# One-core transformer and Hyena block: the value projection computed by token, with key and query preparation under it, and modulation sums closed by a multiplication with ones

## What is computed

```python
mod = c_act @ mod_w[i] + mod_b[i]                      # 12 x 1024 outputs per layer
h_lat = modulate(rms_norm(x, norm_mix_g[i]), sh1, sc1) # 256 x 2048
qa, qb, ka, kb, va, vb = split(h_lat @ w_in)           # queries 2048, keys 512, values 512 columns
qb, kb = rms_norm(qb, q_norm), rms_norm(kb, k_norm)    # per head, only group B
qa, ka, qb, kb = rope(qa), rope(ka), rope(qb), rope(kb)
ka_c, kb_c, va_c, vb_c = split(h_ctx @ w_in[:, Q_WIDTH:])
kb_c = rms_norm(kb_c, k_norm)
```

## Time and profile before

| | |
|---|---|
| median of 3 runs | 2728.9 us (2728.77 to 2733.31) |
| profiled execution, its own time | 2730.95 us |
| its span, first to last instruction | 2729.2 us |
| TensorE busy | 2526.8 us, 93% |
| VectorE busy | 1995.0 us, 73% |
| ScalarE busy | 1120.9 us, 41% |
| data moved by DMA | 608.80 MB, mean 223 GB/s |
| mean granted clock of TensorE | 0.963 of full |

### The profile page before, as it was taken

The page is one execution under the profiler, slowest core; times in us unless marked ns, Lnnn a source line. Parts: engine busy times, 40 slices in busy tenths (PEclk is TensorE's granted clock), DMA queues, the critical chain, the costliest instruction groups (busy, mean ns, idle before and its releaser), DMA issues.

```text
span 2729.2 us, 41835 instructions
## 1 busy us (share of the span) xinstructions
PE 2526.8 (93%) x13492; PEld 2111.7 (77%) x13492; DVE 1995.0 (73%) x2373; ACT 1120.9 (41%) x1494; POOL 0.2 (0%) x4
## 2 busy tenths in 40 slices
PE   7869987797999999999979999999899999999996
PEld 2338884476788888888868788787688888888885
DVE  6788758777987878878768888878675565565654
ACT  2224225643444444444434334233344444444442
POOL 0000000000000000000000000000000000000000
PEclk9989997898999999999999999999899999999998
DMA  8857843474998888888858567576556666666662
GB/s 312 301 187 264 298 159 108 139 259 165 314 311 278 283 278 279 276 283 280 274 172 280 182 226 257 167 252 201 176 181 189 187 190 185 190 186 188 189 185 92
DMA packets 441695, 608.80 MB, mean 223 GB/s; under 512 B 18363, under 2 KB 387228, under 8 KB 439580
## 3 DMA queue, kind: packets, MB, share of 16 engines
q1 hardware_dynamic: 440188, 598.53, 66.9%
q10 hardware_dynamic: 1440, 9.44, 0.9%
HBM read 597.41 MB, written 10.49 MB: 223 GB/s over the span
## 4 chain that ended last, share of the span: by engine, by line
PE 82%; DVE 11%; issue 3%; ACT 2%; DMA 2%; DVEq 0%; SPq 0%; ACTq 0%
PE ps L356 47%; PE ps L365 24%; PE ps L1114 2%; DVE w_lo L395 1%; PE ps L663 1%; PE ps L929 1%; DVE acc L407 1%; PE ps L893 1%; DMA raw<-in_mlp_w 1%; PE ps L1124 1%; DVE hm L715 1%; DVE hm L723 1%; DMA raw<-in_mod_w 1%; DVE lat L729 1%; DVE sm L1508 1%
## 5 line engine op out<-in xcount | busy, mean ns | idle before, releaser
L395 DVE TENSOR_TENSOR w_lo<-raw,w_hi 128x1024 fp32r<-128x1024 f32 x720 | 877.2, 1224 | 523.5 <-ACT w_hi L391 519.3
L391 ACT ACTIVATE w_hi<-raw 128x1024 fp32r<-128x1024 f32 x720 | 760.0, 1060 | 1056.2 <-PE ps L365 892.2
L356 PE MATMUL ps<-lat,w_hi 128*128 128x512 f32 x3200 | 839.2, 399 | 65.6 <-DVE lat L729 58.5
L356 PEld LDWEIGHTS ps<-lat,w_hi 128*128 128x128 f32 x3200 | 587.3, 192 | 177.5 <-issue 49.7
L356 PE MATMUL ps<-alt,w_hi 128*128 128x512 f32 x2688 | 698.2, 395 | 7.8 <-DVE mod L419 5.7
L356 PEld LDWEIGHTS ps<-alt,w_hi 128*128 128x128 f32 x2688 | 488.1, 190 | 96.7 <-DVE mod L419 6.0
L365 PEld LDWEIGHTS ps<-lat,w_lo 128*128 128x128 f32 x3200 | 448.7, 192 | 32.0 <-DVE w_lo L395 0.4
L365 PE MATMUL ps<-lat,w_lo 128*128 128x256 f32 x3200 | 464.1, 284 | 0.0
L365 PEld LDWEIGHTS ps<-alt,w_lo 128*128 128x128 f32 x2688 | 374.7, 191 | 25.8
L365 PE MATMUL ps<-alt,w_lo 128*128 128x256 f32 x2688 | 389.1, 283 | 0.0
L407 DVE SCALAR_TENSOR_TENSOR acc<-slab,silu,acc 128x1024 f32<-128x1024 f32 x300 | 381.4, 1279 | 5.9 <-DMA slab<-in_mod_w 2.4
(11 more groups left out here) (180 smaller groups left out, 1411.6 us busy)
## 6 DMA issues: line engine op xcount, KB each, us to landing
raw<-in_mlp_w SPq DMA_DIRECT2D x512, 512.0 KB, 3.8
slab<-in_mod_w SPq DMA_DIRECT2D x352, 512.0 KB, 6.0
raw<-in_hy_w_in SPq DMA_DIRECT2D x96, 512.0 KB, 6.3
raw<-in_attn_w_in SPq DMA_DIRECT2D x48, 512.0 KB, 6.1
raw<-in_mod_w SPq DMA_DIRECT2D x32, 512.0 KB, 7.4
raw<-in_attn_w_out SPq DMA_DIRECT2D x32, 512.0 KB, 4.8
raw<-in_hy_w_out SPq DMA_DIRECT2D x32, 512.0 KB, 6.6
spec_dram<-spec ACTq DMA_DIRECT2D x8, 1024.0 KB, 7.8
```

What stands on the lines that cost most here:

```text
L356: e.matmul(ps[:, bank, :], w_hi[:, n % RING, kk, fb * P:(fb + 1) * P], t[:, kb, :], start=(kb == 0), stop=False)
L391: e.activation(w_hi[:, n % RING], raw[:, n % RING], ACT.Copy).then_inc(hi_ready, 1)
L395: e.tensor_tensor(w_lo[:, n % RING], raw[:, n % RING], w_hi[:, n % RING].bitcast(F32), ALU.subtract).then_inc(split_ready, 1)
```

## The change

The key projection stays one iteration, T_K. The value projection T_V gets its own loop, `pe_values`: now the token blocks (128 tokens, high or low part) are the stationary operand and the weights stream past, 512 columns at a time. A unit holds 2 feature blocks x 512 columns, is loaded as such, and meets four token blocks in four banks (4, 5, 0, 1); the result has tokens on partitions, as attention needs it, and is copied to `v` by four copies. The transposes of the values and `vt` go. Banks 2, 6 and 7 are free for the preparation of keys and queries, which is hung under the units of T_V by `under_values(n)` on TensorE (n = 1, 2, 4, 5, 6), ScalarE (n = 4, 6, 7) and VectorE (n = 4, 5, 6); its temporaries now lie in `sum_sb` and `lo_sum`. All sums over partitions of `acc` (17 calls of `pe_finish`, four chunks in the start) are now matmuls with a column of ones into one bank: 8 per half, and in the start 8 more per half that add `rows` through a column of the identity. The reductions over the free axis go.

The diff, cut to its core (the body of `under_values` on TensorE is the moved code of L970 to L1004 with its waits and other banks):

```diff
+        k_sq = sum_sb[:].rearrange("p a b t -> p (a b) t")
+        q_sin = lo_sum[:, 0]
...
+        def value_unit(buf, n):
+            return buf[:, n % RING].rearrange("p (k a) n -> p k (a n)", k=2)
+        def sp_values(e, T, w, col, sl):
+            for n in range(8):
+                e.wait_ge(split_ready, 8 * T + n - 3)
+                src = w[2 * n * P:2 * (n + 1) * P, col:col + 4 * HEAD]
+                e.dma_start(value_unit(raw, n), src.rearrange("(k p) n -> p k n", p=P)
+                            ).then_inc(unit_landed[n % RING], 16)
+                if n >= 4:
+                    sp_slabs(e, sl, 1, (n - 4) * 4, 4)
...
+        V_BANKS = (4, 5, 0, 1)
+        def pe_values(e, T, after_unit):
+            for n in range(8):
+                hi, lo = value_unit(w_hi, n), value_unit(w_lo, n)
+                e.wait_ge(hi_ready, 8 * T + n + 1)
+                if n == 0:
+                    e.wait_ge(psum_free, 2 * T_K + 1)
+                for kk in range(2):
+                    kb = 2 * n + kk
+                    for part in range(2):
+                        for tb, bank in enumerate(V_BANKS):
+                            act = (lat, alt)[tb // 2][:, kb, ds(part * TOK + tb % 2 * P, P)]
+                            e.matmul(ps[:, bank, :], act, hi[:, kk, :], start=(kb == 0 and part == 0), stop=False)
+                e.wait_ge(split_ready, 8 * T + n + 1)
+                for kk in range(2):
+                    kb = 2 * n + kk
+                    for tb, bank in enumerate(V_BANKS):
+                        act = (lat, alt)[tb // 2][:, kb, ds(tb % 2 * P, P)]
+                        mm = e.matmul(ps[:, bank, :], act, lo[:, kk, :], start=False, stop=(kb == KB - 1))
+                mm.then_inc(units_done, 1)
+                after_unit(n)
...
-        def pe_finish(e, sl_count, fin, n_acc):
+        def pe_finish(e, sl_count, fin, n_acc, bank=4):
             e.wait_ge(slabs_used, 4 * sl_count + 4)
             e.wait_ge(mod_ready, fin + 1)
             for h in range(n_acc):
                 for b in range(half):
-                    mm = e.transpose(ps[:, 4 + 2 * h + b // 4, (b % 4) * P:(b % 4 + 1) * P],
-                                     acc[:, h, b * P:(b + 1) * P], ident)
+                    at = h * half + b
+                    mm = e.matmul(ps[:, bank, at:at + 1], acc[:, h, b * P:(b + 1) * P], ones[:, 0:1],
+                                  start=True, stop=True)
             mm.then_inc(mod_cols, 1)
...
-        def dve_finish(e, fin, dests):
+        def dve_finish(e, fin, dests, bank=4):
             e.wait_ge(mod_cols, fin + 1)
-            for h in range(len(dests)):
-                ins = e.tensor_reduce(mod_part[:, h], ps[:, 4 + 2 * h:6 + 2 * h, :].rearrange("p a (b k) -> p (a b) k", k=P),
-                                      AX.X, ALU.add)
-            ins.then_inc(mod_summed, 1)
-            e.wait_ge(mod_summed, fin + 1)
             for h, at in enumerate(dests):
-                ins = e.tensor_tensor(mod[:, ds(at, half)], mod_part[:, h], vec("mod_b", at, half), ALU.add)
+                ins = e.tensor_tensor(mod[:, ds(at, half)], ps[:, bank, h * half:(h + 1) * half], vec("mod_b", at, half),
+                                      ALU.add)
             ins.then_inc(mod_ready, 1)
...
+        class Values(Readout):
+            def act_head(self, e, T, g):
+                if g == 1:
+                    e.wait_ge(units_done, 8 * T + 8)
+                    for tb, bank in enumerate(V_BANKS):
+                        e.activation(v[:, tb], ps[:, bank, :], ACT.Copy).then_inc(v_ready, 1)
+                    e.sem_inc(lo_copied, 2)
+            def dve_head(self, e, T, g):
+                if g == 1:
+                    e.wait_ge(v_ready, 4)
+                    e.sem_inc(psum_free, 2)
...
-            sp_call(e, T_KV, 2, a["attn_w_in"], 0, KV_COL, SL_KV)
-            e.wait_ge(split_ready, 8 * (T_KV + 2))
+            sp_iter(e, T_K, a["attn_w_in"], 0, KV_COL, 0, SL_KV)
+            sp_values(e, T_V, a["attn_w_in"], KV_COL + KV_HEADS * HEAD, SL_KV)
+            e.wait_ge(split_ready, 8 * (T_V + 1))
...
-                            e.transpose(ps[:, 4 + 2 * w + b // 4, (b % 4) * P:(b % 4 + 1) * P],
-                                        (acc, acc_odd)[par][:, w, b * P:(b + 1) * P], ident)
-                    for b in range(half):
-                        mm = e.transpose(ps[:, 0, 2 * b:2 * b + 2], rows[:, b * P:(b + 1) * P], ident[0:2, 0:2])
+                            out = ps[:, 4, w * half + b:w * half + b + 1]
+                            e.matmul(out, (acc, acc_odd)[par][:, w, b * P:(b + 1) * P], ones[:, 0:1],
+                                     start=True, stop=False)
+                            mm = e.matmul(out, rows[:, b * P:(b + 1) * P], ident[0:2, w:w + 1],
+                                          start=False, stop=True)
                     mm.then_inc(start_turned, 1)
...
-            with e.Fori(0, 2) as i:
-                pe_iter(e, T_KV + i, lat, lambda j: (norm_ready, 5 + j), alt)
-            e.wait_ge(psum_free, 2 * (T_KV + 2))
-            pe_finish(e, M_ATT, FIN_KV, 2)
+            pe_iter(e, T_K, lat, lambda j: (norm_ready, 5 + j), alt)
+            def under_values(n):
+                if n == 1:
+                    e.wait_ge(psum_free, 2 * (T_K + 1))
...
+            pe_values(e, T_V, under_values)
+            pe_finish(e, M_ATT, FIN_KV, 2, 3)
             e.wait_ge(mod_ready, FIN_KV + 2)
...
-            for h in range(KV_HEADS):
-                for tb in range(4):
-                    mm = e.transpose(ps[:, h, tb * P:(tb + 1) * P], vt[:, h, tb * P:(tb + 1) * P], ident)
-                mm.then_inc(vt_turned, 1)
...
-            act_iter(e, T_KV, r, KeysValues(kt))
-            act_iter(e, T_KV + 1, KeysValues(kt), KeysValues(vt))
-            act_flush(e, T_KV + 1, KeysValues(vt))
-            for h in range(2):
-                e.wait_ge(psum_free, 2 * (T_KV + 2))
-                e.activation(k_sq[:, 2 * h:2 * h + 2, :].rearrange("p a t -> p (a t)"), kt[:, 2 + h, :],
-                             ACT.Square).then_inc(k_squared, 1)
-            for hp in range(4):
-                e.wait_ge(kq_sums, 1 if hp < 2 else hp)
-                e.activation(k_sq[:, 2 * (hp % 2):2 * (hp % 2) + 2, :], q[:, A_HEADS + 2 * hp:A_HEADS + 2 * hp + 2, :],
-                             ACT.Square).then_inc(k_squared, 1)
-            for h in range(KV_HEADS):
-                e.wait_ge(vt_turned, h + 1)
-                e.activation(v[:, h].rearrange("p a d -> p (a d)"), ps[:, h, :], ACT.Copy).then_inc(v_ready, 1)
-            act_root(e, 2, 8)
-            act_root(e, 3, 16)
+            act_iter(e, T_K, r, Keys())
+            def under_values(n):
+                if n == 4:
+                    e.wait_ge(psum_free, 2 * (T_K + 1))
+                    for h in range(2):
+                        e.activation(k_sq[:, 2 * h:2 * h + 2, :].rearrange("p a t -> p (a t)"), kt[:, 2 + h, :],
+                                     ACT.Square).then_inc(k_squared, 1)
+                if n == 6:
+                    act_root(e, 2, 8)
+                if n == 7:
+                    for hp in range(4):
+                        e.wait_ge(kq_sums, 1 if hp < 2 else hp)
+                        e.activation(k_sq[:, 2 * (hp % 2):2 * (hp % 2) + 2, :],
+                                     q[:, A_HEADS + 2 * hp:A_HEADS + 2 * hp + 2, :], ACT.Square).then_inc(k_squared, 1)
+                    act_root(e, 3, 16)
+            act_iter(e, T_V, Keys(), Values(), after_unit=under_values)
+            act_flush(e, T_V, Values())
...
-                    for w in range(2):
-                        ins = e.tensor_reduce(mod_part[:, w], ps[:, 4 + 2 * w:6 + 2 * w, :].rearrange(
-                            "p a (b k) -> p (a b) k", k=P), AX.X, ALU.add)
-                    ins.then_inc(silu_v, 1)
-                    e.wait_ge(silu_v, 4 + c)
-                    e.tensor_tensor(start_part[:, :, ds(half * c, half)], mod_part[:],
-                                    ps[:, 0, 0:2 * half].rearrange("p (b w) -> p w b", w=2), ALU.add).then_inc(start_summed, 1)
+                    for w, dst in enumerate((mod, mod_ctx)):
+                        ins = e.tensor_tensor(dst[:, ds(half * c, half)], ps[:, 4, w * half:(w + 1) * half],
+                                              vec("mod_b", half * c, half), ALU.add)
+                    ins.then_inc(start_summed, 1)
             e.wait_ge(start_summed, 5)
-            for w, dst in enumerate((mod, mod_ctx)):
-                ins = e.tensor_tensor(dst[:, 0:2 * KB], start_part[:, w], vec("mod_b", 0, 2 * KB), ALU.add)
-            ins.then_inc(mod_ready, 1)
-            e.sem_inc(mod_summed, 1)
+            e.sem_inc(mod_ready, 1)
...
+            def under_values(n):
+                if n == 4:
+                    e.tensor_scalar(neg_sink[:], vec("sink", 0, HEADS), -1.0, None, ALU.mult)
```

(37 more changed lines are left out.)

84 lines of the change are left out of this document (45 added, 39 removed).

## The result

| | before | after |
|---|---|---|
| median of the runs | 2728.84 us | 2772.44 us (2769.77 to 2796.62, 4 runs) |
| span of the profiled execution | 2729.2 us | 2772.9 us |
| ratio, 95% interval | | 1.0178 (1.0119 to 1.0237) |

The change makes the kernel slower by 43.6 us between the medians. Forecast were 24.5 us, with a range up to 2767. The direction was right, the size was not, and the time lies outside the range.

What follows compares the result with a forecast made beforehand. TensorE, busy 93% of the span, was taken as the bound. Terms -14.3 - 2.35 - 0.4 + 8.5 + 6 + 27 gave +24.5 us on the 2728.9 us median: 2753 us, range 2724 to 2767.

Steps and rivals of the forecast that it cites:

- The start: Four chunk closings: 64 f32 passes replace 24 transposes and the clock falls, +27 us (5 at held clock, at most 33).
- The half-clock price: Start's closings: after the clock falls, one-column passes are 0.195 us apart, from 1.50 us for 7 loads.
- The load rule: Start's two-row passes: load time goes by the 128 columns, not the depth, so the upper bound 0.115 us was taken.
- (2): Rival for the start: two-row passes are cheap but the clock falls; total +13.5, 2742 us, chance 0.12.
- (4): Rival for the start: cheap rows and held clock together; total -9, 2720 us, chance 0.06.
- One-column passes do not hold the clock: Start's closings: clock falls to half 2.9 us in, so a closing takes 10.5 us instead of 2.55.
- Transposes show no such fall: First MLP's double closing: transposes are followed by a full-speed unit, 2.09 us for eight passes.
- Rival (1): Clock holds under one-column passes: start +5, total -2, 2727 us, same or faster; chance 0.19.
- Value projection and tail: Preparation moved under dense value units and a shorter tail bring the first query swap earlier: -14.3 us (-16.5 to -10).
- rival (3): Value projection: late slabs delay unit 7 and the query squares, TensorE waits 5 us or more; +29, 2758 us, chance 0.08.
- Closings elsewhere: Ones replace transposes behind the start: first MLP +8.5, Hyena +6, ahead of attention output projection -2.35, behind queries -0.4 us.
- Hyena +7.6: Four Hyena closings between a wait of 3.4 us and the first unit: +6 us, bounds 3.2 and 10.6.

Runs made afterwards that it cites:

- e7: Changed kernel with the two-row operand of the start's closings filled with zeros to 128 rows, order and pairs kept: 2764.7 us.
- e5: Changed kernel with the start's 128-row closing matmuls first and the two-row ones after them, in columns of their own: 2769.6 us.
- e9: Changed kernel with 128-column passes in every closing but the one behind the values, start's two-row operand zero-filled to 128 rows: 2721.72 us.
- e1: Changed kernel with transposes and VectorE sums put back in the start's four closings: 2732.44 us, 0.9996 of the kernel before.
- e2: Changed kernel with transposes back in every closing except the one behind the values, leaving the value change: 2716.15 us, 0.9942 of the kernel before.
- e10: e2 with the preparation of keys and queries moved from between the value units to behind them: 2729.33 us, 0.9991 of the kernel before.

## Why the prediction was off, by its own steps

- **The start (+27, measured +43.1): the step that failed.** Its term was the price of a pass. For the two-row passes two bounds were given, 0.06 and 0.115 us; the true spacing in this order, 0.155, lay above the upper one. The upper bound came from passes that all had the same shape, and nothing in the trace showed 128-row and two-row loads in turn. That it was called a bound was the mistake: a row of the same kind in another order is a neighbour, not a limit. The half-clock price was too low as well: the 0.195 came from 7 loads in 1.50 us, a stretch that holds the fall itself, while L1002's 16 loads in 3.49 us are 0.21 apart, which e7 confirms; in the mixed order it is 0.254. By the step's own form: 19 passes at 0.155 and 45 at 0.254 are 14.4 us, where 10.5 stood. The second closing, at half clock from its first pass, took another 2 us that no term had. The other parts held: the clock fell some 2.9 us into the first closing as said, L996 began at half clock (6.35 us instead of 3.70, forecast +3), VectorE's wait shrank from 2.86 to about 0.6.
- **The load rule.** Grouped two-row loads cost what 128-row loads cost, 0.215 and 0.21 us at half clock, and with that the cheap-row rivals (2) and (4) fall. The section LDWEIGHTS of the Trainium skill ("TensorE: Matmul & The Clock Gate") says that the time goes by the 128 columns and not by the depth. e5 and e7 agree for loads of one kind; what the change from one kind to the other costs (0.257 us apart instead of 0.21, at half clock) is not in it.
- **The clock.** "One-column passes do not hold the clock" held in the start, in the closing behind the values and in the first MLP's double closing; the six single closings there, 16 passes of 1.7 us, kept it (the unit behind takes 2.09 us). Hyena does not tell: of its four closings one ran at 1.00 with one-column passes, and e9's wide passes in the same places ran at 0.50 to 0.60. "Transposes show no such fall" was read from one place. The first closing of e1, with the wait behind it, has a granted clock of 0.61 (columns as for e9), and its 24 transposes take 3.3 us instead of 2.55 (the next matmul starts at 55.96, 2.86 of it waiting):

```profile
49.77:56.00 6.23, 3.37 (x25) 2.96 (x26) 2.72 (x4) 0.00 (x0) 0.00 (x0) 0.61 1.00 394
```

  So transposes do not hold it in the start either; there are only fewer of them. The Trainium skill's section "Part 4: PE-mode transpose" ("TensorE: Matmul & The Clock Gate") says that transposes do not count as busy for the clock. The place in e1 agrees, while the double closing of e2 (full speed behind 16 transposes) shows no harm from them in a dense stream.
- **Rival (1), held clock,** did not happen. e9 comes near its condition, with wide passes of 128 rows, and takes 2722 us in one run; (1) said 2727.
- **Value projection and tail (-14.3, measured -13.1).** The mechanism and the size were right, and e10 shows that the move carries most of it. The profiled execution had two stretches of half clock there (416 to 421 us, and in the closing); in e1, where the projection had none, the last matmul ends 52.6 us after the first (forecast 53.3) and the tail takes 4.1 (forecast 4.4). Against the 73.2 us of the kernel before (342.16 to 415.33) that is -16.5; forecast without a fall -15.7. The wait for the squares was 0.36, forecast 0.4; rival (3) did not come.
- **Closings elsewhere.** Ahead of the attention output projection -2.4 (forecast -2.35). A single closing in the first MLP costs 0.92 us more (forecast 0.95), the double one 3.08 (forecast 2.0 plus a clock fall with a chance of one half, which came); together 8.6 against 8.5. That is partly luck: the unit behind the double closing took 1.6 us longer on top of this, which cost nothing, because TensorE had waited 1.95 us for VectorE's `alt` a little later (up to 785.46 in the kernel before) and has no such wait there in the changed one. The stage's other 2.4 us lie ahead of the double closing: from the first unit to it, it takes 103.25 us before and 105.65 after, but also 104.2, 106.6 and 106.6 in e1, e2 and e10, so that is scatter and not the change. Hyena +7.6 (forecast 6, bounds 3.2 to 10.6): 1.7, 0.9, 1.6 and 2.2 us at its four closings, the rest around them.
- **The range** reached to 33 us for the start because it was built from the two wrong pass prices. With the measured 14.4 us a closing as its outer case the start's bound is 43 and the range's end 2777, which holds the result.

## What to carry to other kernels

Move small matmuls under a dense stream of large ones: that gave 13 us here, at a price of 0.11 us a pass, and in e1 and e2 with the clock kept. Do not trade transposes for matmuls on the engine that bounds, unless the engine that is relieved was the last one waited for; 32 f32 matmuls are 64 passes. Where a run of small matmuls stands alone, try full rows and wide moving operands, which cost nothing extra per pass here and took 7.4 us where the mixed one-column passes took 14.5 to 16.5, and do not mix operands of different row counts.

## What the runs showed of the hardware

- Loads of 128-row and two-row f32 operands in turn are 0.155 us apart at full and 0.257 at half clock; 128-row ones alone 0.11 and 0.21, two-row ones alone 0.215 at half clock (e5). Whether two neighbours add into one column makes no difference.
- A granted clock of 1.00 held through 7.4 us of f32 matmuls of 128 rows and 128 columns at 0.115 us each. In one closing of four it fell 1.2 us in and came back before the closing ended. Under the same matmuls with one column, or with two rows in every other one, it was low in every closing after at most 3 us and did not come back within it. What the clock follows stays open.
- With wide passes at half clock the mixture is dearer still: 20.70 us for 57 loads, 0.36 each, where one-column passes in the same order took 0.257. Why is not shown.
